# Block-sparse attention heads: steps of two heads on alternating halves of the array, the compressed branch for all heads at once, scaling on POOL

## What is computed

```python
sc = einsum('bqghd,bngd->bghqn', qg, k_cmp) * scale        # 31 compressed keys
p_cmp = softmax(where(cmp_end <= t, sc, NEG)) * any(valid)
o_cmp = einsum('bghqn,bngd->bqghd', p_cmp, v_cmp)
...                                                        # selected blocks: with 512 tokens all of them
p_sel = softmax(where(key_pos <= t, ss, NEG)); o_sel = p_sel @ v_sel
p_w   = softmax(where(valid_w, sw, NEG));      o_win = p_w @ v_w
out = einsum('bsch,bschd->bshd', gates, o)                 # three gates per head and token
```

## Time and profile before

| | us |
|---|---|
| median of 3 runs | 2533.39 (2528.71 to 2534.61) |
| the profiled execution, its own time | 2534.2 |
| its span, first to last instruction | 2532.4 |
| TensorE busy in the span | 2453.5 (97%) |
| VectorE / ScalarE / POOL busy | 1315.4 / 819.3 / 203.4 |
| mean granted TensorE clock | 0.978 |

### The profile page before, as it was taken

How to read it: one execution, slowest core, us unless ns; L and a number is a source line. 1 busy time by engine, 2 the same in 40 slices (tenths; PEclk the granted TensorE clock), 3 DMA queues, 4 the chain that set the end, 5 groups by cost and what they waited for, 6 DMA issues and landing times. The chain is left out here.

```text
span 2532.4 us, 28747 instructions
## 1 busy us (share of the span) xinstructions
PE 2453.5 (97%) x11404; PEld 1909.7 (75%) x11404; DVE 1315.4 (52%) x2191; ACT 819.3 (32%) x1342; POOL 203.4 (8%) x190
## 2 busy tenths in 40 slices
PE   7999999999999999989999999999999999999998
PEld 6778788768888878866788888877645456888887
DVE  4766455454444443368555454644466663545553
ACT  2333544233222222257432222321433442322222
POOL 1301320000000000023100000101200000000001
PEclk8999999999999999989999999999899999999999
DMA  4233114213333322300123333332200002233331
GB/s 131 75 101 91 34 59 150 75 51 91 95 97 96 96 92 83 92 25 1 42 83 98 94 100 92 92 98 73 84 1 1 1 1 59 86 98 93 99 96 46
DMA packets 290981, 188.08 MB, mean 74 GB/s; under 512 B 7840, under 2 KB 284576, under 8 KB 290848
## 3 DMA queue, kind: packets, MB, share of 16 engines
q1 hardware_dynamic: 290128, 184.31, 24.2%
q10 hardware_dynamic: 720, 1.95, 0.2%
HBM read 184.14 MB, written 2.10 MB: 74 GB/s over the span
## 5 line engine op out<-in xcount | busy, mean ns | idle before, releaser
L464 DVE TENSOR_TENSOR wl<-raw,wh 128x1024 fp32r<-128x1024 f32 x336 | 412.0, 1227 | 753.2 <-ACT wh L454 752.3
L468 PE MATMUL ps<-xb_x,wh 128*128 128x512 f32 (+1 forms) x2000 | 620.9, 392 | 0.0
L454 ACT CAST wh<-raw 128x1024 fp32r<-128x1024 f32 x336 | 349.1, 1040 | 802.9 <-PE ps L468 792.4
L468 PEld LDWEIGHTS ps<-xb_x,wh 128*128 128x128 f32 (+1 forms) x2000 | 373.6, 187 | 79.8
L468 PE MATMUL ps<-xb_x,wl 128*128 128x512 f32 (+1 forms) x1000 | 392.2, 392 | 0.0
L468 PE MATMUL ps<-XH,wh 128*128 128x512 f32 x680 | 274.1, 403 | 3.1 <-DVE mz_prev L1095 2.4
L468 PE MATMUL ps<-XL,wh 128*128 128x512 f32 x680 | 268.5, 395 | 0.0
L468 PE MATMUL ps<-XH,wl 128*128 128x512 f32 x680 | 268.1, 394 | 0.0
L468 PEld LDWEIGHTS ps<-xb_x,wl 128*128 128x128 f32 (+1 forms) x1000 | 187.2, 187 | 44.1
L533 POOL TENSOR_TENSOR sq<-H 128x512 f32<-128x512 f32 x64 | 68.5, 1071 | 1714.0 <-DVE H L583 1636.8
L468 PEld LDWEIGHTS ps<-XH,wh 128*128 128x128 f32 x680 | 130.0, 191 | 31.3 <-DVE mz_prev L1095 3.3
(11 more groups left out here) (329 smaller groups left out, 3649.8 us busy)
## 6 DMA issues: line engine op xcount, KB each, us to landing
raw<-in_mlp_w SPq DMA_DIRECT2D x128, 512.0 KB, 3.7
raw<-in_w_gate_up SPq DMA_DIRECT2D x44, 512.0 KB, 3.7
raw<-in_w_in SPq DMA_DIRECT2D x29, 512.0 KB, 3.6
raw<-in_sb_w_qkv SPq DMA_DIRECT2D x24, 512.0 KB, 3.6
raw<-in_w_down SPq DMA_DIRECT2D x22, 512.0 KB, 3.4
raw<-in_w_out_mix SPq DMA_DIRECT2D x16, 512.0 KB, 3.3
raw<-in_w_kv SPq DMA_DIRECT2D x16, 512.0 KB, 3.8
raw<-in_nsa_w_kv SPq DMA_DIRECT2D x12, 512.0 KB, 3.4
```

The costliest lines, as they stand in the source:

```text
L454: e.copy(shaped(WH[i % NH], i), shaped(RAW[i % NR], i)).then_inc(*w_hi.up(i))
L464: e.tensor_tensor(shaped(WL[i % NH], i), shaped(RAW[i % NR], i), shaped(WH[i % NH], i).bitcast(F), ALU.subtract).then_inc(*w_lo.up(i))
L468: return e.matmul(out, a, b, start=start, stop=stop, skip_group_check=True)
```

## The change

- A step is now a pair of heads c, a block i and one kind (NS has 64 steps: 8 pairs, i = 3 to 0, two kinds). `m` is the head of the pair, and also the half: scores of m = 0 and m = 1 are issued one behind the other into two banks, then both masks. VectorE's and ScalarE's work per step is of the same shape, with m in the place of kind.
- Probabilities are scaled by POOL (`pool_nsa_scale`), which signals the transposes; VectorE only makes reciprocal and gate.
- Values are computed at every step: for each block j of keys, m = 0 and m = 1 in turn, [128 x 64] against 128 queries, into the two halves of the pair's bank. `npts` becomes two rings of four buffers of 512 columns. The bank is opened by the compressed values of both heads at the first step of a pair.
- The compressed branch is done for all heads ahead of the loop: `pe_cmp_scores` issues 64 score matmuls of 31 columns, halves in turn, into four banks of 16 x 32 columns; maximum, subtraction, exponential, sum, reciprocal and gate are done on four tiles of 128 x 512, scaled by POOL (`pool_cmp`); 16 transposes of 128 columns (`pe_cmp_turn`) stand in iterations 1 and 2 of the loop, with their copies shared by ScalarE and VectorE.
- For this the hidden layer of the compression is padded to 32 columns per group, and vc is computed four times, once for each 32 partitions.

```diff
+    NS = [(c, i, kind) for c in range(8) for i in (3, 2, 1, 0) for kind in range(2)]
...
+    def pe_cmp_scores(e):
+        e.wait_ge(*v_made.at("kc"))
+        for ip in range(2):
+            bk = [take(e, ("cz", ip, m)) for m in range(2)]
+            for ii in range(2):
+                i = 2 * ip + ii
+                for c in range(8):
+                    for m in range(2):
+                        mm(e, bk[m][:, 256 * ii + 32 * c:256 * ii + 32 * c + 31],
+                           q_n[64 * m:64 * m + 64, c, 128 * i:128 * i + 128], kc[64 * m:64 * m + 64, c // 2, :],
+                           ii == 0 and c == 0, False)
...
     def pe_nsa_scores(e, n):
...
+        bk = [take(e, ("nz", n, m)) for m in range(2)]
+        for m in range(2):
+            p0 = 64 * m
+            mm(e, bk[m][:, 0:N], qr[p0:p0 + 64, c, 128 * i:128 * i + 128], kd[kind][p0:p0 + 64, g, 0:N], True, False)
+        for m in range(2):
+            mm(e, bk[m][:, N - 128:N], Ib[:, :], maskb[:, 1, :], False, True).then_inc(*scored.up("nz", n, m))
 
     def pe_nsa_turn(e, n):
...
+        for m in range(2):
+            t, p = take(e, ("npt", n, m)), got(("np", n, m))
+            e.wait_ge(*g_made.at("np", n, m))
+            f = turns(e, t, [(128 * j, 128, p[:, 128 * j:128 * j + 128], con("I")) for j in range(i + 1)])
+            f.then_inc(*(turned.up("np", n) if m else turned.up("np0", n)))
 
     def pe_nsa_values(e, n):
...
+        if n % 8 == 0:
...
+            r = 32 * (c % 4)
+            for m in range(2):
+                mm(e, o[64 * m:64 * m + 64, :], vc[r:r + 32, g, :], ptc[r:r + 32, 2 * m + c // 4, :], True, False)
+        e.wait_ge(*a_made.at("npt", n, 0))
+        e.wait_ge(*v_made.at("npt", n, 1))
+        pt = [got(("npts", n, m)) for m in range(2)]
+        for j in range(i + 1):
+            for m in range(2):
+                f = mm(e, o[64 * m:64 * m + 64, 128 * i:128 * i + 128], vs[kind][:, j, 64 * g:64 * g + 64],
+                       pt[m][:, 128 * j:128 * j + 128], False, n % 8 == 7)
+        f.then_inc(*mixed.up("nv", n))
...
         for g in range(4):
             for m in range(2):
...
+                for r in range(0, 128, 32):
+                    f = mm(e, t[r:r + 32, 64 * g:64 * g + 64], hdn[:, 1, m, g, :], w2[:, 1, m, 0, :],
+                           g == 0 and m == 0, m == 1)
...
+        pe_cmp_scores(e)
+        for n in range(NN + 4):
+            if n < NN:
+                pe_nsa_scores(e, n)
+            if n in (1, 2):
+                pe_cmp_turn(e, n - 1)
+            if 3 <= n < NN + 3:
+                pe_nsa_turn(e, n - 3)
             if n >= 4:
                 pe_nsa_values(e, n - 4)
...
+    def pool_nsa_scale(e, n):
+        w, N = got(("nm", n)), 128 * (NS[n][1] + 1)
+        e.wait_ge(*v_made.at("ng", n))
+        for m in range(2):
+            p = got(("np", n, m))
+            e.tensor_scalar(p[:, 0:N], p[:, 0:N], w[:, 8 + m:9 + m], None, ALU.mult).then_inc(*g_made.up("np", n, m))
...
+        for n in range(5):
+            if n < 4:
+                dve_cmp_max(e, *CM[n])
+            if n >= 1:
+                dve_cmp_gate(e, *CM[n - 1])
+        e.memset(ptc[:, :, 0:31], 0.0).then_inc(*v_made.up("ptz"))
...
+        for n in range(NN + 3):
+            if n < NN:
+                dve_nsa_scores(e, n)
...
+            if 1 <= n <= NN:
+                dve_nsa_gates(e, n - 1)
             if n >= 3:
                 dve_nsa_copy(e, n - 3)
```

More of the change, by code:

```diff
@@ L2060, in program @@
     kd = [pk.sb("ks", [128, 4, S]), pk.sb("kw", [128, 4, S])]
[L2061 removed]
+    ptp = Phase(PH0, "nt")
+    npts = [Ring([Buf(ptp.sb(f"pts{m}{i}", [128, S])) for i in range(4)]) for m in range(2)]
+    ptc = Phase(PH0 + 8 * S * 8, "nc").sb("ptc", [128, 4, S])
     qr = Phase(r4, "nq").sb("qr", [128, 8, S])
@@ L2194, in pe_nsa_scores, with pe_cmp_turn @@
+    def pe_cmp_turn(e, cc):
+        for m in range(2):
+            t = take(e, ("cpt", m, cc))
+            for ip in range(2):
+                e.wait_ge(*g_made.at("cp", ip, m))
+            f = turns(e, t, [(128 * i, 128, got(("cp", i // 2, m))[:, 256 * (i % 2) + 128 * cc:256 * (i % 2) + 128 * cc + 128],
+                              con("I")) for i in range(4)])
+            f.then_inc(*turned.up("cp", m, cc))
     def pe_nsa_scores(e, n):
-        h, i = NS[n]
-        g, c, p0 = h // 4, h // 2, 64 * (h % 2)
+        c, i, kind = NS[n]
+        g, N = c // 2, 128 * (i + 1)
@@ L2197, in pe_nsa_scores @@
         e.wait_ge(*g_made.at("rot", "q", c))
[L2198 to L2211, removed]
@@ L2213, in pe_nsa_turn @@
-    def pe_nsa_turn(e, n):
[L2214 to L2227, removed]
@@ L2229, in pe_nsa_values @@
-    def pe_nsa_values(e, n):
[L2230 to L2236, removed]
-            e.wait_ge(*a_made.at("tok", "nv1", 3))
[L2238 to L2244, removed]
+        e.wait_ge(*g_made.at("rot", "k", kind, g))
@@ L2320, in act_nsa_copy @@
     def act_nsa_copy(e, n):
[L2321 to L2333, removed]
+        N = 128 * (NS[n][1] + 1)
+        d = take(e, ("npts", n, 0))
+        e.wait_ge(*turned.at("np0", n))
+        e.copy(d[:, 0:N], got(("npt", n, 0))[:, 0:N]).then_inc(*a_made.up("npt", n, 0))
     def act_nsa(e):
@@ L2377, in out @@
         def out(c):
-            e.wait_ge(*mixed.at("nv", 2 * c + 1))
+            e.wait_ge(*mixed.at("nv", 8 * c + 7))
             act_hi(e, X, "no", c, got(("no", c))[:, :])
[L2381 to L2388, removed]
-                e.wait_ge(*v_made.at("nmax", n))
[L2390 to L2393, removed]
+        for ip, m in CM:
+            p = got(("cp", ip, m))
+            e.wait_ge(*v_made.at("cz", ip, m))
+            e.activation(p[:, :], p[:, :], ACT.Exp, scale=0.125).then_inc(*a_made.up("ce", ip, m))
+        for n in range(NN + 3):
+            if n < NN:
+                N, w = 128 * (NS[n][1] + 1), got(("nm", n))
+                e.wait_ge(*v_made.at("nmax", n))
+                for m in range(2):
+                    p = take(e, ("np", n, m))
+                    e.activation(p[:, 0:N], got(("nz", n, m))[:, 0:N], ACT.Exp, bias=w[:, 2 + m:3 + m],
+                                 scale=0.125, accum_out=w[:, 4 + m:5 + m]).then_inc(*a_made.up("nz", n, m))
+            if n in (1, 2):
+                e.wait_ge(*turned.at("cp", 0, n - 1))
+                e.wait_ge(*v_made.at("ptz"))
+                e.copy(ptc[:, n - 1, 31:S], got(("cpt", 0, n - 1))[:, 31:S]).then_inc(*a_made.up("cpt", 0, n - 1))
             if n >= 3:
                 act_nsa_copy(e, n - 3)
[L2396 to L2399, removed]
+            if n >= 12 and (n - 4) % 8 == 0:
+                out((n - 4) // 8 - 1)
         out(7)
@@ L2410, in act_nsa, with dve_cmp_max, dve_cmp_gate, pool_cmp @@
         a_.end("ns")
-    def dve_nsa_scores(e, n):
[L2413 to L2424, removed]
-        for kind in range(2):
-            e.wait_ge(*scored.at("nz", n, kind))
-            f = e.reduce_max(w[:, kind:kind + 1], got(("nz", n, kind))[:, 0:N], AX.X)
+    def dve_cmp_max(e, ip, m):
+        t, p, w = by_head(got(("cz", ip, m))), by_head(take(e, ("cp", ip, m))), cmpw[:, 2 * ip + m, :]
+        e.wait_ge(*scored.at("cz", ip, m))
+        e.tensor_reduce(w[:, 0:16], t, AX.X, ALU.max).then_inc(*v_made.up())
+        e.wait_ge(*v_made.now())
+        e.tensor_tensor(p, t, w[:, 0:16].unsqueeze(2).to_broadcast([128, 16, 32]), ALU.subtract).then_inc(
+            *v_made.up("cz", ip, m))
+    def dve_cmp_gate(e, ip, m):
+        p, w = by_head(got(("cp", ip, m))), cmpw[:, 2 * ip + m, :]
+        e.wait_ge(*a_made.at("ce", ip, m))
+        e.tensor_reduce(w[:, 16:32], p, AX.X, ALU.add).then_inc(*v_made.up())
+        e.wait_ge(*v_made.now())
+        e.reciprocal(w[:, 32:48], w[:, 16:32]).then_inc(*v_made.up())
+        e.wait_ge(*v_made.now())
+        e.tensor_tensor(w[:, 48:64].rearrange("p (i c) -> p i c", i=2), w[:, 32:48].rearrange("p (i c) -> p i c", i=2),
+                        gat[:, 2 * ip:2 * ip + 2, m:16:2], ALU.mult).then_inc(*v_made.up("cg", ip, m))
+    def pool_cmp(e, ip, m):
+        p, w = by_head(got(("cp", ip, m))), cmpw[:, 2 * ip + m, :]
+        e.wait_ge(*v_made.at("cg", ip, m))
+        e.tensor_tensor(p, p, w[:, 48:64].unsqueeze(2).to_broadcast([128, 16, 32]), ALU.mult).then_inc(
+            *g_made.up("cp", ip, m))
+    def dve_nsa_scores(e, n):
+        w, N = take(e, ("nm", n)), 128 * (NS[n][1] + 1)
+        for m in range(2):
+            e.wait_ge(*scored.at("nz", n, m))
+            f = e.reduce_max(w[:, m:m + 1], got(("nz", n, m))[:, 0:N], AX.X)
         f.then_inc(*v_made.up())
@@ L2569, in pool_nsa @@
         g_.end("kv")
+        for ip, m in CM:
+            pool_cmp(e, ip, m)
+        for n in range(NN):
+            pool_nsa_scale(e, n)
+        g_.end("heads_ns")
         for o in range(8):
```

147 lines of the change are left out of this document (64 added, 83 removed).

## The result

The changed kernel takes 2428.5 us (median, 2422.2 to 2431.0) against 2533.4 of the kernel before beside it: ratio 0.959 (95% interval 0.957 to 0.961), 105 us less. Slow executions are left out of all comparisons: of the kernel before one here (2569.9 us) and one beside the later experiments (2569.2), and one of the copy-first kernel (7583.9). I had forecast 57 us less and a range from 2445 to 2522.

The account below looks back on a forecast made before the run. TensorE was taken to bound the block-sparse stage; values beginning at 1865, 181 us of loop, 2 for low-clock values and 5 for the last chain end it at 2053 instead of 2110, giving 2477 us, range 2445 to 2522.

Parts of the forecast that it names:

- What bounds the stage: Block-sparse heads: TensorE sets the pace, 16.93 of 17.30 us a head; time the stage gives up, the run gives up.
- Overlap: Loop matmuls: one pass of a head beside one of the other, scores 3 passes long; 22.3 us a pair, not 28.4.
- The loop: Eight pairs of heads: 24.6 us a pair, 2.3 of it stalls, where two heads took 34.6.
- the same chain: Scores through softmax to ScalarE's copy, holding later scores and transposes: 3.7 us at wide steps, 2.3 at narrow.
- Ahead of the loop: Compressed score block before the loop, at the low clock: 29.4 us and 1 for masks, until 1843.
- The four-fold weights: Before the loop: compressed value weights made four times, 48 more passes costing 3.2 us.
- The filling: Scores, transposes and compressed transposes before first values, at low clock: 12.5 + 4.1 + 4.1 and 1 us; values at 1865.
- The clock: Granted clock 0.50 from 1812 to some 1865, rising behind the first values to about 1.
- Rival (b): Clock stays at 1.2 GHz in the loop: 20 us more a pair, 2617 us if all eight stay low; chance 0.12.
- Rival (a): No overlap between heads in the loop: 28.4 us a pair, 23 us less in all, 2510 us; chance 0.16.
- POOL: Scaling moved from VectorE: 0.74 us at 512 columns, at most 1.8 a step under 3.7 of cover, costing nothing.
- The range: Whole kernel, to hold 0.8: low end from held clock and shorter chain, high end from no overlap; 2445 to 2522 us.

Follow-up runs that it names:

- copy-first kernel: Changed kernel with ScalarE's copy of step n-3 issued ahead of its exponentials of step n; 2417.5 us, ratio 0.956.
- values-apart run: Changed kernel with each step's values issued head by head, all key blocks of the even head first; 2434.3 us, ratio 0.963.
- scores apart: Changed kernel with the even head's mask placed between the two heads' score matmuls of a step; 2464.3 us, ratio 0.974.
- compressed scores apart: Changed kernel with the compressed score block issued per bank pair as 16 even-head matmuls, then 16 odd-head ones; 2438.1 us, ratio 0.964.
- all apart: Changed kernel with scores, values and compressed scores all issued head by head; 2490.5 us, ratio 0.985.

## Why the forecast was right in direction and short in size

- **What bounds the stage.** Right. TensorE set the pace, the projection behind moved up by what the stage gave up, and no DMA got in the way.
- **Overlap (the step that failed).** "The two passes of one matmul stay in line, since they use the same half. Scores are then 3 passes long instead of 4." The first half is true, the second doesn't follow: the odd head's first pass doesn't wait for the even head's second. It starts beside the first, 0.02 us apart at most, and the even head's passes still queued don't hold it up, as long as they are no more than four. Scores of a pair are about 6.9 us (1.19 at 512 columns with masks, then 0.97, 0.76 and 0.55, twice) instead of 9.0, values 5.6 instead of 6.7, compressed values 1.0 instead of 1.5. The Trainium skill (TensorE: Matmul & The Clock Gate, Part 3) was right that row groups run concurrently; it also says that matmuls start strictly in program order, by which three passes in line would follow. The values-apart run speaks against it where halves differ: with one pass of overlap at the border the step of 4 + 4 passes would have taken 7 passes' time, and it took 4, as in turn (0.60 us); the step of 8 + 8 would have taken 15, and it took 12.
- **The loop.** With the measured pass times in place of mine, the same stepping with the same chain gives about 22 us a pair; measured 21.98. By starts the work of a pair fell from my 22.3 to 18.9, and the stalls rose from 2.3 to 3.0 (the trace's idle column, which counts from modelled ends, has 2.2). The chain and its place were right (all waits stand in front of transposes and are put down to ScalarE's copy), and taking the copy out of it gave the 21.0 of the reckoning. The term was 24.6, 2.6 too much, 21 us over eight pairs. One entry was added up wrong without effect: TensorE's fifth stretch beside the chain is 1.0 + 2.7 + 1.0 = 4.7 by my own terms, not 4.4, and the chain there is 3.0 either way.
- **Ahead of the loop.** 30.4 us for the compressed block became 13.4, because I had given the halves no overlap there at all, though I gave it to them in the loop: 17 us. Some 2.5 of the 17 are the clock, which was full until 1811: the first 64 passes took 4.5 us, the second 7.0. The four-fold weights cost nothing instead of 3.2, for the same reason with columns. The filling took 18.1 instead of 21.7. Together 24 us, which with the loop's 21 makes up the 45 us by which the stage is shorter than forecast (198.4 against 243).
- **The clock.** Right that it is low from 1811 on, wrong on what it waits for: I had tied the rise to the first values. It rose in the scores in the changed kernel (1834 to 1836), and some 15 us behind the start of the first values with the scores apart. What goes with the late rise the runs show: with the values apart the clock read 0.50 for some 24 us, as in the changed kernel; with the compressed scores apart for 31, and 3 more after a short rise; with the scores apart for 51; with all apart for 65. So it goes with the order of the scores first, then of the compressed scores, and not with that of the values. Why is open; TensorE also had no gap in that stretch with the scores apart, and 2 us of gaps in the changed kernel. The figure varies by execution, too: in the second trace of the changed kernel the clock rose between 1820 and 1822, after some 17 us, and dipped once more (0.57 from 1824 to 1828). Rival (b), a clock that stays low in the loop, didn't come: 1.00 in every window of the loop.
- **Rival (a), no overlap.** No run is free of overlap. The nearest to it, all apart, takes 27.2 us a pair (28.4 reckoned) and 2490 in all, less than the 2510 that I gave it: there the compressed values still overlap, and the values in part.
- **POOL.** Off by a factor of two (1.56 for 0.74 at 512 columns), since I took a price from an operation of another form. It cost nothing, as said, but the cover of 3.7 us was needed: two scales of 1.56 are 3.1. The far end that I had named, 2 us each with a wait, was near.
- **The range.** It took its low end from a warm clock and a shorter chain, and not from a better overlap than the one assumed. The overlap had a bound from above that I had not worked out: the odd head entirely free gives about 22 us a pair, 21 us less over eight pairs, and the compressed block of 30.4 us halved is 15 less, together some 2441. That bound belonged in the range, and even then the end should have lain lower, for the filling and the four-fold weights overlap as well.

## What to carry to other kernels

Where a contraction of 64 rows or an output of 64 partitions leaves half of the array idle, put two independent pieces on the two halves close behind each other (within four passes of 128 columns here) and price them as one, narrow passes included. When an unmeasured overlap enters a sum, its upper bound is "the second piece is free", and the range must reach it. After such a step, look at the order of work on the engine in the softmax chain: moving one copy ahead of the exponentials and sharing the scales was worth another 16 us.

## What the runs showed of the hardware that I had not expected

- Passes on the other half start ahead of their turn: eight queued before them cost 0.5 us, four nothing (1.51, 1.07, 0.60 and 0.37 us for 16, 12, 8 and 4 passes issued head by head; 1.02, 0.80, 0.59 and 0.37 in turn).
- Narrow matmuls, which cost four times their columns, also halve: 64 passes of 31 columns took 7.0 us in turn and 13.0 apart, at the low clock. Four groups of 32 output partitions: 64 passes in 1.10 us where 16 took 1.08.
- TensorE's clock can stay at 1.2 GHz with TensorE busy without a gap for 50 us (scores apart, 1806 to 1856) and 64 (all apart, 1806 to 1870). In the changed kernel it was there for 24 us in one trace and 17 in another, with 1 to 2 us of gaps.
- A POOL multiplication in place of 128 x 512 float32 costs 1.49 to 1.57 us where VectorE doesn't scale, and 1.86 where it scales beside it. The other way round, VectorE's product of 2 columns takes 0.25 us on average while POOL scales both heads and 0.16 while it scales none.
